# Decay and rate products of the recurrence on 64 array rows each, issued together at the head of a turn

## The chip, the cores and the metric

One core of a Trainium2 chip runs the whole program. The metric is the device time of one launch in microseconds (us), the median of three runs. The engines are named as in the profile: PE (matmuls) and PEld (its weight loads), DVE (VectorE), ACT (ScalarE), POOL (GpSimd), SP (which only issues DMAs).

## The reference, cut to what matters

One decoder layer for 1024 new tokens of one sequence and 8 x 8 tokens of eight running sequences, all in float32: RMSNorm, one input projection (1024 to 2816 columns), a convolution group, an RWKV-7 group, an output projection, and a mixture of 32 experts (top 2). The change touches two small products of the RWKV-7 group:

```
r, k, v, wl, al, gl = jnp.split(zs, RWKV_SPLITS, axis=-1)       # wl: 64 columns, al: 64 columns
w_log = -jax.nn.softplus(-(w0 + jnp.tanh(wl) @ w_decay_up)) - 0.5   # 64 x 512 weights
decay = jnp.exp(-jnp.exp(w_log))
a = jax.nn.sigmoid(a0 + al @ w_aaa_up)                              # 64 x 512 weights
kk = k * k_k, normalized per head
S_t = S_{t-1} diag(w_t) + (S_{t-1} (-kk_t)) (kk_t * a_t)^T + v_t k_t^T ;  y_t = S_t r_t   # 8 heads of 64
```

Both products contract over 64 numbers. "Decay product" below is the one with `w_decay_up`, "rate product" (`iclr` in the code) the one with `w_aaa_up`.

## The kernel before, in words

The instructions of every engine are written out by hand in order, with semaphores between them. PSUM is the tile `ps` of 8 banks of 128 x 512 float32, `banks(b)`. Tokens go in NT = 9 tiles: eight of 128 and a last one of 64 (the running sequences).

The input projection (L1639, the loop over q at L1617) writes 22 stripes. Between them `between` (L1571) issues small products; at its step 8 these are `decay(0, 7)` and `iclr(0)`. The tile `zs[:, WA0, :]` holds tanh(wl) on partitions 0 to 63 and al on 64 to 127. So the decay product takes its weights `w_da` with rows 64 to 127 set to zero, and the rate product takes `w_aa` with rows 0 to 63 set to zero (POOL memsets, L812 and L813); each uses all 128 array rows. Decay (L1521) is one matmul with 512 moving columns, whose stationary side is the token tile; the rate product (L1527) is four matmuls of 128 moving columns into bank 6. In the trace a float32 matmul leaves two records, so these show as x2 and x8.

The recurrence is a loop over turns j = 0 to 8 (L1790). In turn j PE starts token tile j and finishes tile i = j - 1. Its order: `gram` with bt (L1672), then `decay(j + 1, 6)`, `to_tokens` of v (L1660), `level_y(i, 4)` (L1651), a wait for `decay_sum` (DVE has read bank 6), `iclr(j + 1)` into bank 6 (turns 0 to 7), `chain_rhs(i, 0)`, `level_x(i, 4)`, `to_tokens` of bt into bank 1, `gram` with kt, `level_y(i, 5)`, and so on to `key_norms(j + 1)` (bank 6 again, L1535), `chain_u`, `chain_s`, `chain_y`, `cumulate(j + 1)` (L1610, banks 0 and 1). Most of these use `heads` (L1646) or loops like it: 64 x 64 blocks of the array, partitions 0 to 63 and 64 to 127 in turn. `cumulate` uses 64 rows and 128 columns, with the two halves of a tile in banks 0 and 1.

DVE in a turn (L2507): `first_level` after gram (L2388, L2389), `decay_add(j + 1)` (L2258: reads the decay product from PSUM, adds w0), `level_masks(i, 4)` (L2410, released by `level_y`, and releasing `level_x`), more work, `masked_k` (L2402, released by gram with kt), `small_blocks` (L2424, L2426: waits for the DMA of L584, which reads back what eight DMAs of L581 wrote after `first_level`), `whole_blocks`, `new_state`, `keys`, `scaled_a_b`. ACT in a turn (L1256): `decay_tanh(j + 1)`, `tok_copy` of v, `iclr_tanh(j + 1)` (L1067, reads bank 6), `rhs_copy`, copies for the levels, and so on. Turn j + 1 cannot start its gram before `scaled_a_b(j + 1)`. After the last turn come the final state (among it `new_states`, L1911, whose code order is: L1917 then L1919 for partitions 0 to 63, then L1917 and L1919 for 64 to 127), the output projection (L1949), routing and the experts.

Of the kernel before, what the change touches and what calls it, by code (L numbers as in the profile page):

```python
# [10 lines left out]
ALU = mybir.AluOpType  # L11
# [3 lines left out]
P = 128  # L15
# [6 lines left out]
NT = SEQ // P + 1  # L22
# [49 lines left out]
def hybrid_decoder_step(nc, x_prompt, x_sample, state_conv, state_shift, state_wkv, norm1_g, w_in, conv_w, conv_b,  # L72
# [5 lines left out]
    with ctx:  # L78
# [36 lines left out]
        w0_all, w_da, w_g = (late[:, k * C:(k + 1) * C] for k in range(3))  # L115
# [24 lines left out]
        zs = at(O_ZS, ZT, N)  # L140
# [51 lines left out]
        lw = take(C)  # L192
# [167 lines left out]
        def banks(b, n=1):  # L360
            return ps[:, b:b + n, :].rearrange("p b n -> p (b n)")
# [55 lines left out]
        def level_count(i, k, c):  # L417
            return 4 * i + 2 * (k - 4) + c + 1

        def bonus_bank(i):  # L420
            return 5 if i < NT - 2 else 0

# [333 lines left out]
        def _(pool):  # L756
            step = [0]

            def link(ins):
                step[0] += 1  # L760
                ins.then_inc(pool_chain, 1)
                pool.wait_ge(pool_chain, step[0])
# [46 lines left out]
            for hp in range(CT):  # L809
                link(pool.memset(head_sel[0:64, hp, 2 * hp:2 * hp + 1], 1.0))  # L810
                link(pool.memset(head_sel[64:128, hp, 2 * hp + 1:2 * hp + 2], 1.0))
            link(pool.memset(w_da[64:128, :], 0.0))  # L812
            link(pool.memset(w_aa[0:64, :], 0.0))  # L813
            link(pool.memset(head_back[:, :, :], 0.0))
            for hp in range(CT):
                select(head_back[:, hp, :], ALU.not_equal, 2 * hp, -1, [[1, 2], [0, 64]], 1.0)
# [635 lines left out]
        def _(pe):  # L1452
# [65 lines left out]

            def decay(j, b):
                r = tokens_of(j)  # L1520
                pe.matmul(banks(b)[0:r, :], zs[:, WA0, j * P:j * P + r], w_da, start=True, stop=True)\  # L1521
                    .then_inc(decay_psum, 1)

            def iclr(j):
                r = tokens_of(j)
                for hp in range(CT):
                    ins = pe.matmul(banks(6)[:, hp * P:hp * P + r], w_aa[:, hp * P:(hp + 1) * P],  # L1527
                                    zs[:, WA0, j * P:j * P + r], start=True, stop=True)
                ins.then_inc(iclr_psum, 1)

            def key_norms(j):
# [39 lines left out]
            def between(j):  # L1571
                if j == 0:
                    conv_tails(0)
                if j == 1:
                    conv_tails(1)
                if 3 <= j <= 6:
                    key_squares(j - 3)
                if j == 4:
                    conv_tails(2)
                if j == 6:  # L1580
                    conv_tails(3)
                if j == 8:
                    pe.wait_ge(tanh_done, 1)
                    pe.wait_ge(tail_copied, 4)
                    decay(0, 7)
                    pe.wait_ge(knorm_root, 1)
                    iclr(0)
                if j == 9:
                    conv_mean(0)
                if j == 10:  # L1590
                    pe.wait_ge(iclr_done, 1)
                    key_norms(0)
                    conv_mean(1)
                if j == 11:
                    conv_var(0)
                if j == 12:
                    conv_var(1)
# [57 lines left out]
            def to_tokens(j, b, src):  # L1655
                for c in range(chunks_of(j)):
                    for hp in range(CT):
                        for p in (0, 64):
                            h = slice(p, p + 64)
                            ins = pe.matmul(banks(b)[h, (c * CT + hp) * 64:(c * CT + hp + 1) * 64],  # L1660
                                            src[h, hp, c * 64:c * 64 + 64], ident[h, h], start=True, stop=True)
                ins.then_inc(tok_psum, 1)
# [105 lines left out]
            def sample_inverse(n):  # L1768
                low, high = banks(6)[:, 0:256], banks(6)[:, 256:512]
                if n == 0:  # L1770
                    pe.wait_ge(pt_done, NT)
                    for hp in range(CT):
                        for p in (0, 64):
                            h = slice(p, p + 64)
                            ins = pe.matmul(low[h, hp * 64:hp * 64 + 64], inv_u[h, hp, :], ident[h, h], start=True,
                                            stop=True)
                else:
                    pe.wait_ge(s8_in, n)
                if n == 1:
                    heads(low, inv_v, inv_u, alone=True)  # L1780
                    ins = heads(high, inv_u, inv_v, alone=True)
                if n == 2:
                    heads(low, inv_v2, inv_p, alone=True)
                    ins = heads(high, inv_u2, inv_v2, alone=True)
                if n == 3:
                    pe.wait_ge(blk_done, 2 * NT - 1)
                    ins = heads(low, inv_v4, inv_x2, alone=True)
                ins.then_inc(inv8_psum, 1)

            for j in range(NT):  # L1790
                i = j - 1
                r = tokens_of(j)
                pe.wait_ge(prod_done, j + 1)
                pe.wait_ge(ar_done, j + 1)
                pe.wait_ge(gk_done, j)
                gram(j, bt, gb_psum)
                if j == 0:
                    pe.wait_ge(zs_done, ZT - 1)
                    to_tokens(j, 0, zs[:, V0:V0 + CT, 0:P])
                    to_tokens(j, 1, bt)  # L1800
                    pe.wait_ge(z_ready, ZT)
                    conv_mean(2)
                if j < NT - 1:
                    pe.wait_ge(kk_done, 2 * j + 1)
                    decay(j + 1, 6)
                if j:
                    to_tokens(j, 0, zs[:, V0:V0 + CT, j * P:j * P + r])
                    if j >= 2:
                        pe.wait_ge(rk_used, j - 1)
                    if j >= 4:  # L1810
                        pe.wait_ge(mix_done, j - 3)
                    level_y(i, 4)
                if j < NT - 1:
                    pe.wait_ge(decay_sum, j + 2)
                    iclr(j + 1)
                else:
                    sample_inverse(0)
                if j:
                    chain_rhs(i, 0)
                    level_x(i, 4)  # L1820
                if j:
                    to_tokens(j, 1, bt)
                if j == NT - 1:
                    sample_inverse(1)
                pe.wait_ge(prod2_done, j + 1)
                pe.wait_ge(gb_done, j + 1)
                gram(j, kt, gk_psum)
                if j:
                    level_y(i, 5)
                pe.wait_ge(tok_done, 3 * j + 1)  # L1830
                to_tokens(j, 0, kt)
                if j < NT - 1:
                    pe.wait_ge(iclr_done, j + 2)
                    key_norms(j + 1)
                else:
                    sample_inverse(2)
                if j:
                    level_x(i, 5)
                if j >= 3:
                    pe.wait_ge(tok_done, 3 * j + 2)  # L1840
                    to_channels(j - 3, 1)
                if j == NT - 1:
                    state_in(0)
                if j:
                    chain_u(i, 0)
                    if j == NT - 1:
                        pe.wait_ge(tok_done, 3 * NT)
                    bonus(i)
                    chain_s(i, 0)
                    if j == NT - 1:  # L1850
                        sample_inverse(3)
                    chain_y(i, 0)
                    if j == NT - 1:
                        state_in(1)
                    chain_rhs(i, 1)
                if j < NT - 1:
                    pe.wait_ge(tok_done, 3 * j + 3)
                    if j >= 3:
                        pe.wait_ge(aff_done, j - 2)
                    cumulate(j + 1)  # L1860
                if j == 0:
                    conv_var(2)
                if j == NT - 1:
                    state_in(2)
                if j:
                    chain_u(i, 1)
                if j >= 3:
                    gate(j - 3, 4)
                if j == NT - 1:
                    state_in(3)  # L1870
                if j:
                    chain_s(i, 1)
                    chain_y(i, 1)
# [295 lines left out]
        def _(dve):  # L2169
# [84 lines left out]
            def decay_add(j):  # L2254
                r = tokens_of(j)
                dve.wait_ge(decay_psum, j + 1)
                dve.wait_ge(c_psum, j)
                dve.tensor_tensor(lw[0:r, :], banks(6 if j else 7)[0:r, :], w0_all[0:r, :], ALU.add).then_inc(decay_sum, 1)  # L2258

            def keys(j):  # L2260
                r = tokens_of(j)
# [685 lines left out]
```

## Time and profile before

| | |
|---|---|
| time, median of 3 runs | 1171.45 us (1171.27 to 1173.0) |
| the profiled execution, its own time | 1171.15 us |
| its span, first to last instruction | 1169.4 us |
| PE busy | 1107.1 us, 95% |
| DVE, ACT, POOL busy | 673.3, 366.7, 223.0 us |
| mean granted TensorE clock | 0.979 |

```profile
## 2 busy tenths in 40 slices
PE   6999999999998799999999999986999999999987
PEld 4666666666666688898995455544333333333342
DVE  6288999993554687888753332456334343433417
ACT  6000011111222656777651221122132223222334
POOL 7000000010001212333220001002233333342110
PEclk9999999999999899999999999987999999999999
```

Each digit stands for 29.2 us. The projection is slices 2 to 12, the recurrence slices 13 to 21, the output projection runs to slice 26, routing is slice 27, and the experts follow. PEclk is the granted clock in tenths (9 is 90% or more).

### The profile page before, as it was taken

The page shows a single profiled execution, that of the slowest core. Times are in us where ns is not written, and L with a number is a line of the kernel's source. Part 1 is how long each engine was busy: PE and PEld are TensorE (multiplying, and loading weights), DVE is VectorE, ACT ScalarE, POOL GpSimd, SP SyncE. Part 2 cuts the span into 40 slices and gives each one's busy share as a digit, 9 for nine tenths or more (in the row PEclk, how much of TensorE's full clock was granted, in tenths as well). Part 3 has the DMA queues.
Part 4 walks back from the last instruction along what each step waited for, and adds up shares of the span by engine and source line. Part 5 has one row for each costly group of instructions (what it writes and reads, how often), then busy time and mean ns, then how long its engine had stood idle before and what let it go on. Part 6 is the DMA issues. An engine that isn't in the chain of part 4 may idle for free.

```text
span 1169.4 us, 24207 instructions
## 1 busy us (share of the span) xinstructions
PE 1107.1 (95%) x9388; PEld 667.8 (57%) x9389; DVE 673.3 (58%) x1143; ACT 366.7 (31%) x720; POOL 223.0 (19%) x280
## 2 busy tenths in 40 slices
PE   6999999999998799999999999986999999999987
PEld 4666666666666688898995455544333333333342
DVE  6288999993554687888753332456334343433417
ACT  6000011111222656777651221122132223222334
POOL 7000000010001212333220001002233333342110
PEclk9999999999999899999999999987999999999999
DMA  9211111110000111111133321148898889999839
GB/s 291 73 36 36 37 37 33 30 43 23 1 1 6 16 16 22 18 19 18 23 93 140 120 77 47 45 152 337 347 368 319 314 318 336 415 408 405 334 110 400
DMA packets 97292, 171.42 MB, mean 147 GB/s; under 512 B 44377, under 2 KB 68624, under 8 KB 87921
## 3 DMA queue, kind: packets, MB, share of 16 engines
q1 hardware_dynamic: 89713, 152.31, 36.5%
q0 software_dynamic: 7488, 17.84, 4.3%
q8 instruction: 65, 1.06, 0.4%
q14 instruction: 26, 0.21, 0.1%
HBM read 153.63 MB, written 25.91 MB: 154 GB/s over the span
## 4 chain that ended last, share of the span: by engine, by line
PE 82%; DVE 9%; DMA 5%; ACT 2%; issue 1%; SPq 1%; POOLq 0%; DVEq 0%; ACTq 0%
PE ps L1639 27%; PE ps L2099 14%; PE ps L1949 10%; PE ps L2129 7%; PE ps L1651 6%; PE ps L1672 3%; PE ps L2086 2%; DMA arena<-in_w_exp_up_dram 2%; DVE arena L2436 2%; PE ps L2164 1%; PE ps L1660 1%; PE ps L1979 1%; DMA arena<-in_w_exp_down_dram 1%; DVE arena L2439 1%; PE ps L1527 1%
## 5 line engine op out<-in xcount | busy, mean ns | idle before, releaser
L1639 PE MATMUL ps<-arena 128*128 128x384 f32 (+1 forms) x1040 | 319.1, 468 | 0.0
L1639 PEld LDWEIGHTS ps<-arena 128*128 128x128 f32 x1040 | 196.9, 190 | 119.0 <-issue 1.9
L2099 PE MATMUL ps<-arena 128*64 x416 | 188.5, 596 | 3.0 <-DVE arena L2853 1.3
L2102 PE MATMUL ps<-arena 128*64 128x512 f32 x416 | 188.5, 596 | 0.0
L2250 DVE SCALAR_TENSOR_TENSOR arena<-arena,cw 128x1024 f32<-128x1024 f32 x240 | 168.3, 779 | 0.4
L2099 PEld LDWEIGHTS ps<-arena 128*64 128x64 f32 x416 | 54.4, 136 | 111.8 <-issue 111.7
L1949 PE MATMUL ps<-arena 128*128 128x512 f32 x256 | 113.1, 596 | 0.0
L1651 PE MATMUL ps<-arena 64*64 64x64 f32 x2960 | 99.9, 219 | 5.9 <-DVE arena L2450 1.7
L2129 PE MATMUL ps<-arena 128*64 x208 | 96.5, 607 | 2.4 <-ACT arena L1407 2.4
L1651 PEld LDWEIGHTS ps<-arena 64*64 64x64 f32 x2960 | 93.0, 135 | 9.4 <-issue 4.7
L2132 PE MATMUL ps<-arena 128*64 128x512 f32 x208 | 96.5, 607 | 0.0
L1949 PEld LDWEIGHTS ps<-arena 128*128 128x128 f32 x256 | 47.5, 190 | 57.1 <-issue 57.0
L848 POOL COPY lastz<-arena 128x1 f32<-128x1 f32 x14 | 11.4, 815 | 313.0 <-ACT arena L1123 313.0
L1117 ACT ACTIVATE arena<-ps 128x768 f32<-128x768 f32 x14 | 11.4, 812 | 186.3 <-PE ps L1639 186.3
L942 POOL DMA_INDIRECT late<-xn_rows,g_idx x24 | 63.7, 2655 | 20.4 <-POOL g_idx L939 20.4
L2853 DVE COPY arena<-arena 128x4096 f32 x26 | 59.4, 2285 | 8.5 <-SPq L683 6.8
L2838 DVE TENSOR_TENSOR small<-ps,small 128x256 f32<-128x256 f32 x26 | 11.1, 426 | 89.7 <-ACT small L1391 89.7
L2129 PEld LDWEIGHTS ps<-arena 128*64 128x64 f32 x208 | 26.8, 138 | 53.1 <-issue 53.1
L2862 DVE COPY arena<-ps 128x256 f32<-128x256 f32 x26 | 11.0, 424 | 77.9 <-PE ps L2115 77.9
L1407 ACT ACTIVATE arena<-arena 128x2048 f32 x26 | 49.6, 1908 | 18.5 <-SPq L687 17.3
L2102 PEld LDWEIGHTS ps<-arena 128*64 128x64 f32 x416 | 54.4, 136 | 0.0
L2320 DVE TENSOR_TENSOR arena<-arena 128x1024 f32<-128x1024 f32 x14 | 17.1, 1224 | 49.5 <-ACT arena L1123 49.5
(364 smaller groups left out, 1526.8 us busy)
## 6 DMA issues: line engine op xcount, KB each, us to landing
arena<-in_w_exp_gate_dram SPq DMA_DIRECT2D x32, 1024.0 KB
arena<-in_w_exp_up_dram SPq DMA_DIRECT2D x32, 1024.0 KB
arena<-in_w_exp_down_dram SPq DMA_DIRECT2D x32, 1024.0 KB, 10.1
arena<-in_w_in_dram SPq DMA_DIRECT2D x22, 512.0 KB, 4.1
arena<-in_x_prompt_dram SPq DMA_DIRECT2D x16, 512.0 KB, 8.1
arena<-y_rows SPq DMA_DIRECT2D x8, 1024.0 KB, 16.9
arena<-in_w_out_dram SPq DMA_DIRECT2D x2, 2048.0 KB, 10.7
xn_rows<-arena SPq DMA_DIRECT2D x8, 512.0 KB, 2.8
```

What stands on the lines that cost most here:

```text
L942: pool.indirect_dma_start(out=xg[b], out_offset=None, in_=xn2_rows, in_offset=bass.IndirectOffsetOnAxis(ap=g_idx[b][:, :], axis=0), bounds ...
L1407: act.activation(wd.rearrange("p c n -> p (c n)"), wring[:, bass.ds(slot, 1), 2 * DC * F:].rearrange("p a n -> p (a n)"), ACT.Copy)\
L1639: ins = pe.matmul(banks(proj_bank(q) + piece)[:, 0:n1 - n0], win[q % 6][:, c, :], xnT[:, c, n0:n1], start=(c == 0), stop=(c == DC - 1))
L1651: ins = pe.matmul(dst[h, hp * 64:hp * 64 + 64], lhs[h, hp, :], rhs[h, hp, :], start=alone or (first and hp == 0), stop=alone or last, skip ...
L1672: ins = pe.matmul(banks(2 + c)[h, hp * P:(hp + 1) * P], lhs[h, hp, t], AR[j % 3][h, hp, :, t], start=True, stop=True)
L1949: ins = pe.matmul(banks(2 * (i % 2) + half)[0:r, :], lhs, wout[c // CT][:, c % CT, half * 512:half * 512 + 512], start=(c == 0), stop=(c = ...
L2099: pe.matmul(banks(b)[0:HS, :], xgT[b][:, c, 0:HS], wring_gu[:, bass.ds(slot, 1), 0:2, c, :].rearrange("p a w f -> p (a w) f"), start=(c == ...
L2102: ins = pe.matmul(banks(b)[HS:P, :], xgT[b][:, c, HS:P], wgu[b][:, :, c, :], start=(c == 0), stop=(c == DC - 1))
L2129: pe.matmul(banks(5 + half)[0:HS, :], hT[:, c, 0:HS], wring[:, bass.ds(slot, 1), n0:n0 + 512].rearrange("p a n -> p (a n)"), start=(c == 0 ...
L2132: ins = pe.matmul(banks(5 + half)[HS:P, :], hT[:, c, HS:P], wd[:, c, half * 512:half * 512 + 512], start=(c == 0), stop=(c == 1))
L2250: dve.scalar_tensor_tensor(out=dst, in0=src, scalar=w, in1=dst, op0=ALU.mult, op1=ALU.add).then_inc(conv_tap, 1)
L2853: dve.tensor_copy(wgu[b].rearrange("p w c f -> p (w c f)"), wring[:, bass.ds(slot, 1), 0:2 * DC * F].rearrange("p a n -> p (a n)"))\
```

## The change

`decay` and `iclr` take 64 rows each: the decay product rows 0 to 63 of tokens and weights, the rate product rows 64 to 127. The two memsets that made the other halves zero are gone. In turns 1 to 7 `iclr(j + 1)` stands right behind `decay(j + 1)`, and the decay product goes to bank 1 (tiles 2 and up), so that it isn't in the bank of the rate product; tile 0 keeps bank 7, tile 1 keeps bank 6. Turn 0 keeps its old order. The wait for `decay_sum` moves to where bank 1 is written next, ahead of `to_tokens(j, 1, bt)`, and turn 1 gets a wait for `cvar_done`, whose order the old wait had implied.

```
+        def decay_bank(j):
+            return (7, 6)[j] if j < 2 else 1
...
-            link(pool.memset(w_da[64:128, :], 0.0))
-            link(pool.memset(w_aa[0:64, :], 0.0))
...
-                pe.matmul(banks(b)[0:r, :], zs[:, WA0, j * P:j * P + r], w_da, start=True, stop=True)\
+                pe.matmul(banks(b)[0:r, :], zs[0:64, WA0, j * P:j * P + r], w_da[0:64, :], start=True, stop=True)\
...
-                    ins = pe.matmul(banks(6)[:, hp * P:hp * P + r], w_aa[:, hp * P:(hp + 1) * P],
-                                    zs[:, WA0, j * P:j * P + r], start=True, stop=True)
+                    ins = pe.matmul(banks(6)[:, hp * P:hp * P + r], w_aa[64:P, hp * P:(hp + 1) * P],
+                                    zs[64:P, WA0, j * P:j * P + r], start=True, stop=True)
...
-                    decay(0, 7)
+                    decay(0, decay_bank(0))
...
-                    decay(j + 1, 6)
+                    decay(j + 1, decay_bank(j + 1))
+                    if j:
+                        iclr(j + 1)
...
-                if j < NT - 1:
-                    pe.wait_ge(decay_sum, j + 2)
-                    iclr(j + 1)
-                else:
+                if j == 0:
+                    pe.wait_ge(decay_sum, 2)
+                    iclr(1)
+                if j == NT - 1:
                     sample_inverse(0)
+                if j == 1:
+                    pe.wait_ge(cvar_done, len(PIECES))
...
                 if j:
+                    pe.wait_ge(decay_sum, min(j + 2, NT))
                     to_tokens(j, 1, bt)
...
-                dve.tensor_tensor(lw[0:r, :], banks(6 if j else 7)[0:r, :], w0_all[0:r, :], ALU.add).then_inc(decay_sum, 1)
+                dve.tensor_tensor(lw[0:r, :], banks(decay_bank(j))[0:r, :], w0_all[0:r, :], ALU.add).then_inc(decay_sum, 1)
```

## Rows read from the trace of the kernel before

**Rows 1.** The page's chain that ended last, by engine.
```profile
PE 82%; DVE 9%; DMA 5%; ACT 2%; issue 1%; SPq 1%; POOLq 0%; DVEq 0%; ACTq 0%
```

**Rows 2.** Timeline of PE, turn 4: start, us, line, shapes, xrecords [idle before].
```profile
471.77 1.92 PE L1672 MATMUL ps<-arena 64*64 64x128 f32 x32
473.62 1.12 PE L1521 MATMUL ps<-late,arena 128*128 128x512 f32 x2
474.68 1.15 PE L1660 MATMUL ps<-ident,arena 64*64 64x64 f32 x32
475.66 1.10 PE L1651 MATMUL ps<-arena 64*64 64x64 f32 x32
476.69 1.16 PE L1527 MATMUL ps<-arena 128*128 128x128 f32 x8
477.78 3.02 PE L1651 MATMUL ps<-arena 64*64 64x64 f32 x96
480.62 1.10 PE L1660 MATMUL ps<-ident,arena 64*64 64x64 f32 x32
481.56 1.92 PE L1672 MATMUL ps<-arena 64*64 64x128 f32 x32
483.31 1.10 PE L1651 MATMUL ps<-arena 64*64 64x64 f32 x32
484.24 1.10 PE L1660 MATMUL ps<-ident,arena 64*64 64x64 f32 x32
...
493.23 1.16 PE L1610 MATMUL ps<-small,arena 64*128 64x128 f32 x16
494.32 0.68 PE L1651 MATMUL ps<-arena 64*64 64x64 f32 x16
...
498.72 1.92 PE L1672 MATMUL ps<-arena 64*64 64x128 f32 x32
```

**Rows 3.** Timeline of PE, `new_states` after the recurrence.
```profile
621.49 1.08 PE L1917 MATMUL ps<-arena 64*64 64x512 f32 x4
622.39 1.03 PE L1919 MATMUL ps<-arena,gain 64*64 64x512 f32 x4
623.25 1.07 PE L1917 MATMUL ps<-arena 64*64 64x512 f32 x4
```

**Rows 4.** Timeline of PE, the head of turn 7 (the 64-token tile's products).
```profile
552.60 1.92 PE L1672 MATMUL ps<-arena 64*64 64x128 f32 x32
554.44 1.07 PE L1521 MATMUL ps<-late,arena 128*64 128x512 f32 x2
555.44 1.15 PE L1660 MATMUL ps<-ident,arena 64*64 64x64 f32 x32
```

**Rows 5.** Timeline of PE, tile 0's products inside the projection.
```profile
283.89 1.02 PE L1521 MATMUL ps<-late,arena 128*128 128x512 f32 x2
...
285.63 1.78 PE L1639 MATMUL ps<-arena 128*128 128x384 f32 x5
```

**Rows 6.** Timeline of DVE, turn 4.
```profile
476.34 0.89 DVE L2410 TENSOR_TENSOR arena<-ps,mask_lv 128x256 f32<-128x256 f32 x2 [0.58 <-PE ps L1651]
...
483.52 1.23 DVE L2402 TENSOR_TENSOR arena<-ps,small 128x1024 f32<-128x1024 f32 x1 [2.59 <-PE ps L1672]
...
485.32 0.16 DVE L2424 TENSOR_TENSOR arena<-arena 64x12 f32<-64x12 f32 x1
```

**Rows 7.** Timeline of ACT, turn 4.
```profile
477.88 1.14 ACT L1067 ACTIVATE arena<-ps,prm 128x128 f32<-128x128 f32 x4 [0.23 <-PE ps L1527]
```

**Rows 8.** Timeline of SP, turn 4.
```profile
481.53 0.51 SPq L584 DMA_DIRECT2D arena<-u_blocks  x1
```

**Rows 9.** That DMA among the issues of 480 to 486 us: KB, median us to landing.
```profile
arena<-u_blocks SPq DMA_DIRECT2D x1, 64.0 KB, 2.1
```

**Rows 10.** Timeline of PE, the head of turn 1.
```profile
388.83 3.68 PE L1672 MATMUL ps<-arena 64*64 64x128 f32 x32 [7.49 <-DVE arena L2284]
```

**Rows 11.** Busy us (and x) by engine, granted clock, DMA share, GB/s of a stretch.
```profile
370.00:390.00 20.00, 9.51 (x112) 8.75 (x114) 14.79 (x35) 9.31 (x19) 2.99 (x3) 0.74 0.06 14
```

## The prediction

> **What bounds the kernel now.** I read the chain of waits first: PE carries 82% of it [rows 1], so time taken off PE is worth something only where PE ends last. Then the timeline of PE over one turn of the recurrence [rows 2]. From 471.77 to 484.24 PE idles nowhere: each group starts as the one before lets go, and a turn lasts 498.72 - 471.77 = 26.95 us. Third, the timelines of DVE, ACT and SP over the same turn [rows 6 to 9]: in the stretch that the change touches (the head of the turn, from gram with bt to gram with kt) DVE waits 2.59 us for gram with kt. From there the turn goes on through DVE's block inverse, state update and back to PE; all of that hangs on gram with kt and moves with it. So the head is bound by PE alone, and what it loses the turn loses, up to DVE's 2.59 us.
>
> **What a visit costs now.** I count from start to start, since durations overlap [rows 2]. The decay product stands 474.68 - 473.62 = 1.06 us. The gram before it takes 1.85, the one that is followed by a product of its own shape 483.31 - 481.56 = 1.75, so 0.10 more; the transposes after it take 0.98 against 481.56 - 480.62 = 0.94, so 0.04. Together 1.20 us. The rate product stands 477.78 - 476.69 = 1.09; the 32 records before take 1.03 against 0.93 (484.24 - 483.31), 0.10 more, and the 96 after it 2.84 against 3 x 0.93, 0.05. Together 1.24 us.
>
> What of that is streaming? Four consecutive 512-column passes on one row half took 623.25 - 621.49 = 1.76 us, 0.44 each [rows 3], so decay streams 0.88 us and 1.20 - 0.88 = 0.32, say 0.33, is the change of array shape in and out. The rate product is then 0.91 of streaming (8 x 0.114) and the same 0.33.
>
> **Do two row halves run at once?** `cumulate` sends 16 records of 64 rows, halves alternating, in 494.32 - 493.23 = 1.09 us, exactly what 8 records of 128 rows and the same columns take [rows 2]. So two halves run side by side, each at full-array speed, into separate banks and over all 128 array columns, which is the form that the change uses. But there the halves alternate in the queue. Here decay's second pass stands between its first and the rate product, and uses the same rows as the first. Does the rate product overtake it? `new_states` answers: in its code L1919 for partitions 0 to 63 stands ahead of L1917 for 64 to 127, yet all four L1917 records start before the L1919 ones, and eight passes take the time of four [rows 3]. I take it that each row half works off its own list.
>
> The Trainium skill says otherwise ("TensorE: Matmul & The Clock Gate", "Part 3: Packing small matmuls", under the mechanism): matmuls start and end strictly in program order, and only weight loads are pulled ahead. By that the rate product would wait for decay's second pass to start; this trace disagrees (four L1917 records ahead of L1919). The result by that rule is the first rival.
>
> **Part by part.**
> - Turns 1 to 6 (decay and rate product with 128 tokens): one visit in place of two, 0.33 + the longer of 0.88 and 0.91 = 1.24 us. Saved 1.20 + 1.24 - 1.24 = 1.20 each, 7.2 in all. Bounds: no overlap at all gives 0.33 + 0.88 + 0.91 = 2.12 and saves 0.32; nothing in the rows lets the visit go under the rate product's 1.24, so 1.20 is also the upper end. Half clock at the head of turn 1 [rows 10] doesn't change this, because it is the rate product's visit, after the clock is back, that goes.
> - Turn 7: the stationary side is the 64-token tile, so decay is now 64 x 64 (like gram around it), the rate product 64 x 128. Different shapes: no row shows two shapes side by side, every change of shape in rows 2 costs its tenths. Decay's visit now is 555.44 - 554.44 + 0.09 + 0.04 = 1.13 [rows 4]; after, 0.88 without a change of shape. Saved 0.25; if the shapes did overlap, 1.13. I take 0.25.
> - Tile 0 in the projection: both now stand 285.63 - 283.89 = 1.74 us in a stream of their own shape [rows 5]; after, 0.33 + 0.91 = 1.24. Saved 0.50; without overlap 2.12, a loss of 0.38. PE never idles there, so it counts in full.
> - Turn 0: old order. Decay gets a change of shape, but stands before a wait for DVE's `decay_add`; 0, and if uncovered a loss of 0.33.
> - The two memsets: POOL is done with its constants in the first of the 40 slices, and PE asks for them only behind the first stripe. 0, from 0 to nothing lost.
> - The wait for `cvar_done` in turn 1: DVE writes it before `first_level(1)`, PE asks after gram(1) and two more groups. It was implied before; 0. The wait for `decay_sum` before `to_tokens` of bt: `decay_add` stands ahead of `level_masks`, which has begun at 476.34 [rows 6]; PE gets there after 479. Behind that wait is all of PE, but it is met by over 2 us. 0.
>
> **What comes closer.** The rate product stood between `level_y` and `level_x` and covered DVE's masks. After the change the transposes of v start at about 473.62 + 1.08 = 474.70, `level_y` at 475.68, `chain_rhs` at 476.61 and `level_x` at 477.54. DVE's first mask follows `level_y` and is done at about 476.34 + 0.45 = 476.8: 0.7 to spare. ACT's `iclr_tanh` waited 0.23 us for PE [rows 7]; now it starts that much earlier and no more, since the copy of v stands before it, so `rhs_copy` lags by about a microsecond against PE, but PE wants it only after gram with kt. DVE's wait for gram with kt shrinks from 2.59 to 1.39. The tightest: `small_blocks` starts at 485.32 and its DMA landed at 481.53 + 2.1 = 483.63 [rows 6, 8, 9], 1.69 to spare, 0.49 after. That DMA chain hangs on gram with bt and does not move.
>
> **Sum.** 7.2 + 0.25 + 0.50 = 7.95 us off the profiled execution's own 1171.15 gives 1163.2; that execution stands 0.3 under the median of the runs, so 1163.5. Its own range is 1162 to 1165.5: DMA landings differ by tenths from turn to turn, and a half-clock stretch elsewhere can fall on more or less PE work.
>
> **Rivals.**
> 1. *Matmuls keep program order* (0.20). The rate product starts with decay's second pass: 0.33 + 0.44 + 0.91 = 1.68 a visit, 0.76 saved in six turns = 4.56, turn 7 0.25, tile 0 0.06: 4.87, time 1166.6. For it: nothing in rows 2 decides, since halves alternate there. Against: rows 3.
> 2. *No overlap between products of different length or queue order* (0.07). 0.32 x 6 + 0.25 - 0.38 = 1.8, time 1169.7. Against: `cumulate` in rows 2.
> 3. *Another chain takes over* (0.10). The DMA of the blocks has 1.69 to spare. If it lands a microsecond later than in rows 9, only 0.69 a turn can be had: that gives about 0.69 x 6 + 0.25 + 0.5 = 4.9, time 1166.6. Against: the DVE and SP rows show the room in turn 4.
> 4. *The clock* (0.04), the slower side. After PE idled 7.49 us the gram of turn 1 took 3.68 us against 1.92 [rows 2, 10], and in that stretch the granted clock averaged 0.74 [rows 11]; the low level is half, 1.2 GHz. If thinner work on PE (half-array products, more waiting at the tail) let the clock fall for a stretch, half its length is lost. From 15.9 us of it the gain is gone, from 20.6 us the kernel is slower by over 0.2%; one turn of 27 us gives 1163.5 + 13.5 = 1177.0. Against: in the full turns PE has no gap over a microsecond or two, and `heads` already uses half-array blocks at full clock.
>
> For turn 7 the Trainium skill has a rule ("TensorEngine Tiling (Array Packing)", "Key Properties"): changing the tiling mode drains the array. It fits the tenths in rows 2; were it wrong for two row halves, turn 7 alone would give 0.9 more.
>
> **How the numbers follow.** The forecast has 0.57, the rivals 0.20, 0.07, 0.10 and 0.04, and 0.02 is left for what I don't see. A change under 0.2% (2.3 us) can't be told from none here. The forecast, rival 1 and rival 3 are faster by more (0.87), rival 2 falls within (with part of the rest, 0.09), rival 4 is slower (0.04). The range runs from 1161.5 (all of the forecast's room, a little more in turn 7) to 1167.5 (rivals 1 and 3), leaving out rivals 2 and 4.
>
> **What would show it.** In the timeline of PE after, L1521 x2 and L1527 x8 start within hundredths of each other and the transposes of v start 1.1 us after decay (1.5 to 1.6 under rival 1, 2.0 under rival 2); the turn lasts 25.75 us; DVE's wait before L2402 is near 1.4; no new wait before L2424 or `level_x`. In turn 7 the two follow one another. A turn of 26.2 us with decay's passes half covered would make rival 1 right; full overlap with a turn over 26 us, rival 3.

## The result, and the profile after

The changed kernel takes 1165.95 us (median of 9 runs, 1162.43 to 1170.05), the kernel before 1171.88 in the same comparison; the ratio is 0.9946, 95% interval 0.9932 to 0.9959. By the ratio that is 6.3 us less (the medians differ by 5.9), where 7.95 were forecast; 1163.5 was predicted, with a range of 1161.5 to 1167.5. The profiled execution took 1164.35 us of its own (before: 1171.15), with a span of 1162.6 (1169.4).

First the busy times of its engines, then PE's timeline over the head of turn 4, which answers to [rows 2]. The same code has other line numbers now: gram L1673, decay L1522, rate L1528; DVE's L2402 and L2424 are L2408 and L2430, SP's L581 and L584 are L584 and L587.

```profile
PE 1101.3 (95%) x9388; PEld 667.2 (57%) x9389; DVE 672.4 (58%) x1143; ACT 364.5 (31%) x720; POOL 223.9 (19%) x278
```
```profile
468.89 1.92 PE L1673 MATMUL ps<-arena 64*64 64x128 f32 x32
470.74 0.69 PE L1522 MATMUL ps<-late,arena 64*128 64x512 f32 x1
470.74 0.71 PE L1528 MATMUL ps<-arena 64*128 64x128 f32 x4
471.27 0.59 PE L1522 MATMUL ps<-late,arena 64*128 64x512 f32 x1
471.29 0.61 PE L1528 MATMUL ps<-arena 64*128 64x128 f32 x4
471.83 1.15 PE L1661 MATMUL ps<-ident,arena 64*64 64x64 f32 x32
...
488.38 1.15 PE L1652 MATMUL ps<-arena 64*64 64x64 f32 x32 [0.49 <-DVE arena L2456]
```

Decay's first record and the first rate record start together, and 471.83 - 470.74 = 1.09 us later the transposes of v begin: what the rate product alone took. Decay's second pass starts when four rate records are through, beside the other four.

Turn 7, which answers to [rows 4]: the two products have different shapes and follow one another.

```profile
548.19 1.02 PE L1522 MATMUL ps<-late,arena 64*64 64x512 f32 x2
549.14 1.10 PE L1528 MATMUL ps<-arena 64*128 64x64 f32 x8
550.17 1.15 PE L1661 MATMUL ps<-ident,arena 64*64 64x64 f32 x32
```

The starts of gram with bt, read off the two timelines, give the length of each turn:

| turn | 0 | 1 | 2 | 3 | 4 | 5 | 6 | 7 |
|---|---|---|---|---|---|---|---|---|
| before, us | 24.80 | 29.07 | 26.93 | 26.94 | 26.95 | 26.94 | 26.94 | 26.50 |
| after, us | 25.11 | 27.87 | 25.72 | 25.75 | 26.06 | 25.75 | 25.74 | 26.21 |

Turns 1 to 7 give 7.17 us. Tile 0's visit gives 0.56 (from decay(0) to gram of turn 0: 80.14 before, 79.58 after). That makes 7.73; this execution reached tile 0's products 0.97 later (0.88 of it was lost ahead of the projection, where the granted clock from 15 to 20 us averaged 0.77, before 1.00), turn 0 took 0.31 more, and what follows turn 8's gram took 589.95 in place of 590.30: 6.8 less in all, the difference of the spans.

Turn 4 is the odd one. DVE there ([rows 6] before):

```profile
479.44 1.23 DVE L2408 TENSOR_TENSOR arena<-ps,small 128x1024 f32<-128x1024 f32 x1 [1.36 <-PE ps L1673]
...
481.55 0.17 DVE L2430 TENSOR_TENSOR arena<-arena 64x12 f32<-64x12 f32 x1 [0.22 <-DMA arena<-u_blocks]
```

And the chain of waits of that turn, start, us, what:

```profile
475.01 1.49 SPq L584
476.55 1.52 DMA u_blocks<-arena
478.08 3.44 DMA arena<-u_blocks
481.75 0.18 DVE arena L2432
```

From the end of gram with bt on, PE is off this chain: it runs through DVE's `first_level`, SP's eight DMA issues and the read-back, which here took 3.44 us to land, against 2.1 in [rows 9]. DVE waited, and PE then waited 0.49 for DVE's state, 0.31 more than in the same turn before:

```profile
492.15 1.15 PE L1651 MATMUL ps<-arena 64*64 64x64 f32 x32 [0.18 <-DVE arena L2450]
```

Turn 1 comes out at the forecast 1.20 less, but by two deviations. There the clock returns from its low level at about the same time in both profiles (granted 0.70 from 392 to 394 us, before 0.69), but gram began 0.72 later (389.55 in place of 388.83 us). So decay's visit, which took 393.88 - 392.44 = 1.44 us before, fell in part under the low clock, and the merged visit after did not (394.25 - 393.16 = 1.09):

```profile
394.25 1.15 PE L1661 MATMUL ps<-ident,arena 64*64 64x64 f32 x32
395.54 3.95 PE L1652 MATMUL ps<-arena 64*64 64x64 f32 x128
```

The last line should follow 0.98 after the one before it and follows after 1.29: by the chain of waits `level_y` waited for the DMA that brings the inverted blocks back (L597), which landed at 395.49. So 0.31 was lost again.

### The profile page after: what moved, and what is told of

Same layout as the page of the kernel before. It is cut to its first block, busy times and chain, and to the rows that moved or that the text cites. A ratio compares the mean times of both kernels' runs of the same rounds, so it can differ in the third digit from the quotient of the medians.

```text
span 1162.6 us, 24205 instructions
## 1 busy us (share of the span) xinstructions
PE 1101.3 (95%) x9388; PEld 667.2 (57%) x9389; DVE 672.4 (58%) x1143; ACT 364.5 (31%) x720; POOL 223.9 (19%) x278
## 3 DMA queue, kind: packets, MB, share of 16 engines
q8 instruction: 65, 1.06, 0.4%
## 4 chain that ended last, share of the span: by engine, by line
PE 82%; DVE 8%; DMA 5%; ACT 2%; issue 2%; SPq 1%; POOLq 0%; ACTq 0%; DVEq 0%
PE ps L1640 27%; PE ps L2105 14%; PE ps L1955 10%; PE ps L2135 8%; PE ps L1652 5%; PE ps L1673 2%; PE ps L2092 2%; PE ps L2170 1%; DVE arena L2442 1%; PE ps L1985 1%; PE ps L1661 1%; DMA arena<-in_w_exp_down_dram 1%; DVE arena L2445 1%; DMA arena<-y_rows 1%; PE ps L2121 1%
## 5 line engine op out<-in xcount | busy, mean ns | idle before, releaser
L2105 PE MATMUL ps<-arena 128*64 x416 | 188.5, 596 | 3.2 <-DVE arena L2838 2.0
L2105 PEld LDWEIGHTS ps<-arena 128*64 128x64 f32 x416 | 54.5, 136 | 111.6 <-issue 111.5
L1392 ACT ACTIVATE small<-ps 128x256 f32<-128x256 f32 x26 | 10.0, 383 | 116.5 <-PE ps L2108 116.5
```

What stands on the lines that cost most here:

```text
L2105: pe.matmul(banks(b)[0:HS, :], xgT[b][:, c, 0:HS], wring_gu[:, bass.ds(slot, 1), 0:2, c, :].rearrange("p a w f -> p (a w) f"), start=(c == ...
```

## The experiments

Times vary by 4 to 5 us either way between executions, so beside each ratio I read the profile. The measure is the time from turn 2's gram to turn 8's (six turns, one of them turn 7): 161.20 before, 155.23 after.

**The changed kernel again.**

> The changed kernel itself, for a second profile and for times on the chip of the runs beside it. Theory (row halves side by side, one change of array shape less, the block DMA now with only half a microsecond to spare): 6 to 8 us under the kernel before; in the profile every turn 1 to 6 shows 1.09 us from decay to the transposes of v, and DVE waits for the read-back of the blocks by some tenths in one or more turns, not the same turns as in the first profile. Rival (the spread of its times comes from where the half-clock stretches fall, not from that DMA): turns of one length in both profiles, and the difference sits outside the recurrence.

Median 1164.75, ratio 0.9939 (0.9918 to 0.9959). Six turns: 155.17. Turns 2 to 7 took 25.84, 25.74, 25.90, 25.75, 25.74 and 26.20. Turn 4 is the longest of the full ones again: the read-back landed at 477.89 + 2.94 = 480.83, and DVE's `small_blocks` (L2430) started at 480.85, about 0.15 later than its masks alone would have let it. The wait that was expected is there, smaller and in the same turn. It explains 0.3 and 0.15 us, not the spread; the rival is right on that. In turn 1 the low clock lasted into the merged visit here, which took 393.96 - 392.16 = 1.80 us, and the turn took 28.21, only 0.86 less than before. Where the spread sits the other profiles show: behind turn 8's gram, in code that no kernel here changes, the spans are 587.8 to 595.4 us over 14 profiles, and the changed kernel's own two differ there by 2.1. The end of the output projection differs by 1.4 us between them, the stretch from the first to the last of the experts' matmuls at L2105 by 4.5 (304.2 to 308.7); the cause stays open.

**64 rows, but old order and old banks** (only the halves: `zs[0:64, ...]` with `w_da[0:64, :]`, `zs[64:P, ...]` with `w_aa[64:P, ...]`).

> 64 rows each, but old order and old banks. Theory: nothing is side by side in turns 1 to 6, each visit costs what it cost (1.20 and 1.24 us), so 0 there; tile 0 in the projection is adjacent already and in two banks, so 0.6 less, turn 7 0.25 less: 0.9 us under before, about 1171. Rival (half-row products are cheaper by themselves): 2 us or more under before.

Ratio 1.0006 (0.9989 to 1.0022). Six turns: 160.92 (the 0.28 less is turn 7's), and turn 4's head is that of before within a hundredth per step:

```profile
473.57 1.12 PE L1519 MATMUL ps<-late,arena 64*128 64x512 f32 x2
474.63 1.15 PE L1658 MATMUL ps<-ident,arena 64*64 64x64 f32 x32
...
476.64 1.16 PE L1525 MATMUL ps<-arena 64*128 64x128 f32 x8
477.72 1.49 PE L1649 MATMUL ps<-arena 64*64 64x64 f32 x43
```

A half-row product is no cheaper by itself: 1.06 and 1.08 us. Tile 0's two products, which were neighbours in two banks already, did overlap: 285.18 - 284.09 = 1.09 us, as expected.

**New order and banks, but 128 rows** (the two memsets are back).

```
-    zs[0:64, WA0, ...], w_da[0:64, :]          +    zs[:, WA0, ...], w_da
-    w_aa[64:P, ...], zs[64:P, WA0, ...]        +    w_aa[:, ...], zs[:, WA0, ...]
```

> New order and banks, but 128 rows each with the zeroed halves as before. Theory: one change of shape less per turn and no overlap, a visit of 2.12 in place of 2.44, 0.32 in each of 7 turns: 2.2 us under before, about 1169.5. Rival (the new order frees other engines earlier and that is the gain): 5 us or more under before.

Ratio 0.9981 (0.9963 to 0.9999). Six turns: 159.35. Turns 2 to 6 took 26.6 each, 0.34 less than before, turn 7 0.14 less.

```profile
475.06 1.12 PE L1524 MATMUL ps<-late,arena 128*128 128x512 f32 x2
476.02 1.05 PE L1530 MATMUL ps<-arena 128*128 128x128 f32 x8
477.00 1.15 PE L1663 MATMUL ps<-ident,arena 64*64 64x64 f32 x32
```

1.94 us for both. So one change of shape less is worth a third of a microsecond a turn and the overlap the other 0.85 (26.60 - 25.75); in the recurrence neither half of the change gives the overlap alone.

**Both products on one row half** (`w_da[0:64, ...]` and `zs[0:64, ...]` for the rate product too).

> The changed kernel, but the rate product reads rows 0 to 63 of the token tile and the decay weights, so that both products use the same row half (its rates are then not the reference's). Banks, order, sizes and shape stay. Theory (it is the other row half that lets them run together): they follow one another, 0.88 + 0.91 + 0.2 of shape change, 2.0 us from decay to the transposes of v, 0.9 more than in the changed kernel in each of 6 turns, 6 us in all. Rival (the separate banks and the adjacency bring the overlap): 1.1 us as in the changed kernel.

One run: 1172.71 (before beside it 1174.48). Six turns: 159.37. Its turn 1 took 32.25 us, with a granted clock of 0.76 from 390 to 416 us, so the total is no measure here.

```profile
477.80 1.12 PE L1522 MATMUL ps<-late,arena 64*128 64x512 f32 x2
478.76 1.05 PE L1528 MATMUL ps<-arena,late 64*128 64x128 f32 x8
479.74 0.45 PE L1661 MATMUL ps<-ident,arena 64*64 64x64 f32 x8
```

1.94 us again. Order, banks, sizes and shape are those of the changed kernel; without the other row half there is no overlap, and separate banks and adjacency don't bring it. Whether the banks of these two have to differ was not tried.

**The rate product ahead of decay** (`iclr(j + 1)` before `decay(j + 1, ...)`).

> The changed kernel with the rate product ahead of the decay product in turns 1 to 7. Theory (each row half works off its own list of matmuls, so the order of two halves in the queue says nothing): the two start within hundredths of each other again, 1.09 us from there to the transposes of v. Rival (matmuls start in program order): decay starts only with the last of the rate product's records, 0.8 us later, and the visit is 1.7 us or more.

One run: 1167.35 (before: 1174.48). Six turns: 157.43.

```profile
471.21 0.82 PE L1528 MATMUL ps<-arena 64*128 64x128 f32 x5
471.77 0.69 PE L1522 MATMUL ps<-late,arena 64*128 64x512 f32 x1
471.87 0.50 PE L1528 MATMUL ps<-arena 64*128 64x128 f32 x3
472.30 0.59 PE L1522 MATMUL ps<-late,arena 64*128 64x512 f32 x1
472.82 1.15 PE L1661 MATMUL ps<-ident,arena 64*64 64x64 f32 x32
```

Theory and rival were both wrong. Decay did overtake three records, but only from the fifth rate record on: 1.61 us a visit. "Each row half works off its own list" is too wide. Decay's first record is ninth in the queue and starts with the fifth; in `new_states` [rows 3] the fifth starts with the first. That suggests a reach of four records.

**Two and three of the four rate matmuls ahead of decay.**

```
                     if j:
                         iclr(j + 1, range(2))          # or range(3)
                     decay(j + 1, decay_bank(j + 1))
                     if j:
                         iclr(j + 1, range(2, CT))      # or range(3, CT)
```

> The changed kernel with two of the four rate matmuls (4 records) ahead of decay, two behind. With all four ahead, decay started with the rate product's fifth record, not its first. Theory now: a matmul of the free row half is started if it is at most four records behind the one that runs (as in new_states and in the run with all four ahead). So here decay, five places from the front, starts with the first rate record, and the visit is 1.09 us. Rival (only a matmul right behind is reached): decay starts with the third or fourth rate record, and the visit is 1.3 us or more.

> Three of the four rate matmuls (6 records) ahead of decay, one behind. Theory (reach of four records): decay starts with the third rate record, about 0.3 us into the visit with the shape change, and the visit is 1.35 us. Rival (a reach that isn't counted in records): the same start as with two or with four ahead.

One run each: 1165.17 and 1170.69 (before: 1170.74). First with two ahead, then with three:

```profile
470.48 0.37 PE L1528 MATMUL ps<-arena 64*128 64x128 f32 x1
470.50 0.69 PE L1522 MATMUL ps<-late,arena 64*128 64x512 f32 x1
...
471.57 1.15 PE L1662 MATMUL ps<-ident,arena 64*64 64x64 f32 x32
```
```profile
471.11 0.60 PE L1528 MATMUL ps<-arena 64*128 64x128 f32 x3
471.44 0.69 PE L1522 MATMUL ps<-late,arena 64*128 64x512 f32 x1
...
472.49 1.15 PE L1662 MATMUL ps<-ident,arena 64*64 64x64 f32 x32
```

1.09 and 1.38 us. Fifth in the queue, decay starts with the first; seventh, with the third (0.33 in). Six turns: 155.41 and 157.89; in the second DVE also waited for the read-back of the blocks, 0.23 us in turn 2 and 0.60 in turn 6, so its six turns are not the price of the order alone. The reach of four records holds in all four places in which it was seen, though only for this pattern, and the single times of these runs stand inside the spread.

**Both products in 64 x 64 blocks, like their neighbours.**

```
+                for t in range(0, r, 64):
+                    ins = pe.matmul(banks(b)[t:t + 64, :], zs[0:64, WA0, j * P + t:j * P + t + 64], w_da[0:64, :], ...)
...
+                    for p in (0, 64):
+                        ins = pe.matmul(banks(6)[p:p + 64, hp * P:hp * P + r], w_aa[64:P, hp * P + p:hp * P + p + 64], ...)
```

> Both products in the 64 x 64 shape of their neighbours: decay as two matmuls (64 tokens each, rows 0 to 63), the rate product as eight (64 channels each, rows 64 to 127). Theory: four blocks each work off their own list, a visit is 0.88 to 0.91 with no change of shape, 0.35 less in turns 1 to 6 and 1.2 less in turn 7, up to 3.3 us under the changed kernel; but the block DMA has only 0.49 us to spare, so DVE waits for it in most turns and 1 us or more of this is lost: 1161 to 1163. Rival (two column halves of one row half share its stream and take turns): a visit of 1.8, 0.6 more than in the changed kernel, 3 us or more over it.

Ratio 0.9975 (0.9958 to 0.9992), median 1168.62 where 1161 to 1163 was expected; all twelve times lie above the six of the changed kernel beside them (1162.91 to 1165.73). Yet turns 3 to 7 took 25.36, 25.43, 25.37, 25.50 and 25.03 us, as expected. Within the recurrence the loss is turn 2, of 29.03 us. SP and DVE there:

```profile
421.98 5.28 SPq L584 DMA_DIRECT2D u_blocks<-arena  x8
430.29 0.51 SPq L587 DMA_DIRECT2D arena<-u_blocks  x1
```
```profile
432.42 0.16 DVE L2433 TENSOR_TENSOR arena<-arena 64x12 f32<-64x12 f32 x1 [2.03 <-DMA arena<-u_blocks]
```

PE and its clock:

```profile
439.23 1.88 PE L1655 MATMUL ps<-arena 64*64 64x64 f32 x32 [2.40 <-DVE arena L2459]
```
```profile
436.00:445.00 9.00, 5.25 (x96) 4.73 (x90) 6.75 (x13) 3.22 (x8) 1.25 (x2) 0.81 0.15 25
```

One of SP's eight issues took 2.08 us (the others 0.30 to 0.43), the write issued last landed after 3.45 us (of the eight the median is 1.8), and only then could the read-back be issued. DVE waited 2.03 us for it, PE idled 2.40 us, and after that idling the granted clock fell to its low level (1.2 GHz): 0.50 from 440 to 442 us, 0.81 on average over the stretch above. The 32 records took 1.88 us in place of 1.15. In turn 1 DVE waited 0.45 us for the read-back too. Six turns: 155.72; with turn 2 at 25.4 like the others it would be 152.1. This accounts for the gain that is missing, but not for a kernel slower than the changed one: the six turns are only 0.5 us over the changed kernel's, and 5.4 of the 6.8 us by which this profile's span exceeds it stand behind turn 8's gram. That part stays open.

**The same, with two of the eight block DMAs issued by ACT** (SP issues `diagonal[:6]`; ACT, ahead of `decay_tanh`, waits for `pt_done` and issues the last two).

> Both products in the 64 x 64 shape, and two block DMAs by ACT. Theory: turns 1 to 6 at 25.4 us and turn 7 at 25.0 with no wait on the block DMA, so the 3 us that the shape saves stay: about 1162. Rival (the 3.4 us stretch at half clock in turn 2 came from the thinner work of the products, not from the wait on the DMA): the stretch is there again without a wait, and the time stays at 1166 to 1169.

Ratio 0.9933 (0.9909 to 0.9957), median 1164.72. No wait for the read-back, no fall of the clock in turn 2, turns 2 to 5 at 25.35 to 25.37 us. Turn 6 took 26.53: PE waited 0.95 us for `x_blocks`, the blocks' way back, a wait that turn 6 of the changed kernel does not show. Six turns: 153.00, 2.2 less than the changed kernel. So the thin work by itself did not bring the clock down; the idling after the late DMA came before the fall, as far as two profiles show. The time of about 1162 that was expected was not reached; behind turn 8's gram this profile has 593.9 us, 4.0 more than the changed kernel's first.

**The changed kernel with two block DMAs by ACT.**

> The changed kernel with two of the eight block DMAs of a turn issued by ACT (ahead of its decay_tanh) in place of SP. Theory (the DMA chain of the blocks is what is left of 0.49 us of room): SP's last issue comes about 0.9 us earlier, no wait of DVE on it in any turn, turns 1 to 6 all 25.75 us; at most some tenths under the changed kernel, about 1164.5 to 1165. Rival (two DMAs on ACT delay its copies): turns longer by 0.2 or more.

Ratio 0.9942 (0.9920 to 0.9965), median 1164.31; every turn from 2 to 6 25.74, six turns 154.91. ACT's two issues in turn 4, no cost to PE:

```profile
471.36 0.85 ACTq L1263 DMA_DIRECT2D u_blocks<-arena  x2
```

**The kernel before with two block DMAs by ACT.**

> The kernel before, with two of the eight block DMAs by ACT. Theory: there they have 1.6 us or more to spare, so 0 (within 0.2%). Rival (the earlier landing is worth something by itself, or ACT's copies are late): 1 us or more either way.

Ratio 0.9989 (0.9970 to 1.0008; one execution of 4628 us is not in it), six turns 161.20, as before. The relief is worth nothing while there is room.

**Only the 64-token tile's rate product in 64 x 64 blocks.**

> The changed kernel, with the rate product of the 64-token tile alone in 64 x 64 blocks (turn 7, where decay already has that shape). Theory: the two now run side by side there and no shape changes, turn 7 shrinks from 26.2 to 25.0 us, about 1 us under the changed kernel, less what its block DMA has of room. Rival (two products of different line and length in one shape still follow one another): turn 7 at 25.9.

Ratio 0.9953 (0.9932 to 0.9973), which can't resolve a microsecond. Turn 7 went from 26.21 to 25.20 us. Its head:

```profile
548.91 0.59 PE L1522 MATMUL ps<-late,arena 64*64 64x512 f32 x1
548.92 0.62 PE L1530 MATMUL ps<-arena 64*64 64x64 f32 x13
```

Here decay and thirteen rate records run side by side, and three more rate records had started beside gram's last ones: with one shape throughout no time is lost between the products.

By the ratios none of the versions with 64 x 64 blocks or with ACT's DMAs is shown faster than the changed kernel: their intervals all reach into its own.

## Why the prediction was right, and where it was off

- *A visit of 1.20 us disappears in turns 1 to 6*: right. 1.20, 1.21, 1.19, 0.89, 1.19, 1.20 measured, 6.88 of 7.2. The new visit is 1.09 from start to start, and 1.23 with its edges, where 1.24 was computed. For turn 1 the reason given (the half clock changes nothing, since the visit that goes comes after it) is wrong: what the low clock reaches now is the merged visit, in part or not at all. Its 1.20 is luck, a visit at the high level and a new wait of 0.31; in the second profile the turn saved 0.86.
- *Turn 7, 0.25*: 0.29. That different shapes don't overlap was a choice between 0.25 and 1.13, and the right one; with one shape the turn gave another 1.0 (forecast 0.88).
- *Tile 0, 0.50*: 0.56 from tile 0's decay to turn 0; the visit itself went from 1.74 to 285.94 - 284.85 = 1.09 us, 0.65 less, where 1.24 was put for it.
- *Two row halves run at once*: right, and separated from order, banks and shape by three runs (1.94, 1.94 and 1.08 + 1.06 against 1.09 us).
- *Each row half works off its own list*: this step is wrong as it was put. The rows read for it show an overtaking of three records, no more, and the reach is four. The change stands inside it, since decay's second pass is the only thing to be overtaken, so no number suffered. Rival 1 (strict program order) is wrong too.
- *The tightest is the DMA of the blocks, 0.49 to spare*: right as to which. The 0.49 was read off one turn. In the first profile of the changed kernel the room was 0.25 to 0.87 us in the turns other than 4, since the read-back landed after 2.1 to 3.0 us there. It took 0.3 us of turn 4 in one profile and 0.15 in the other; rival 3 held in one turn of each, and there only in part.
- *No new wait at `level_x`, before `to_tokens` of bt, or for `cvar_done` in turn 1*: none in either profile. Not thought of was `level_y` in turn 1, 0.31 for the blocks' way back in the first.
- *The size*: the profiled pair gave 6.8 of 7.95, the ratio 6.3, that of the repeat 7.2. The recurrence and tile 0 gave 7.73 and, in the second profile, the six turns were even shorter. The rest is not in the steps: 0.97 us of it was lost before tile 0's products in this execution, and the stage behind turn 8 differs between executions by more than the whole remainder. The forecast set one execution's span against the median, and gave itself 1162 to 1165.5 for that; the median of nine stands half a microsecond above that and 2.45 above 1163.5. Of this 0.43 is the kernel before, whose own median rose from 1171.45 to 1171.88.

## What to carry to other kernels

Two products with a contraction over 64 rows cost one if they stand on different row halves, have the same block shape and stand within a few matmuls of each other in the queue. Of the 1.2 us a turn, one row half for both took back 0.85, the old place and bank all of it, decay four matmuls behind 0.5, and in turn 7 different shapes about 1.0. Decay and rate product wrote different banks wherever they overlapped, over the same partitions; whether they must was not tried. `new_states` [rows 3] overlaps within one bank, but on different partitions. Giving up the zero padding alone was worth nothing in the recurrence. Count the changes of block shape too: 0.3 us a visit, and a product that can take its neighbours' shape saves them. When PE's head shrinks, look up which DMA round trip was timed against it: room of 1.7 us became 0.5 by the sum and 0 to 0.9 as measured, and in the run with the next 0.35 us a turn to gain PE idled 2.4 us and had a stretch at low clock in one turn.

## What the runs showed of the hardware

- A matmul on a free row half overtook others in the queue and started up to four records ahead of its place: the fifth with the first (`new_states`, and two rate matmuls ahead of decay), the seventh with the third, the ninth with the fifth.
- Four 64 x 64 blocks of the array took decay, the rate product and the end of the gram before side by side. From the start of gram to the transposes of v it took 444.12 - 441.51 = 2.61 us in the run with ACT's DMAs, beside 471.83 - 468.89 = 2.94 in the changed kernel.
- Eight small DMA issues of SP took 3.63 to 4.75 us in turns 1 to 7 of the kernel before, 4.54 to 4.92 in the changed one's first profile, and 5.28 in one turn (above). The 64 KB read-back landed after 2.1 to 2.8 us before and 2.1 to 3.4 in that profile. Turn 4 of the kernel before, from which the room was read, had some of its shortest issues (3.64 us). A chain with half a microsecond to spare meets a slow turn now and then.

- The time of the stages that all these kernels share varied by up to 7.6 us between executions (587.8 to 595.4), more than the change's 6.3.
